# Modulation pieces loaded at once, routing steps put in another order, and the first expert piece drawn ahead, in a two-layer hybrid backbone kernel

## The reference, cut to what matters

```python
for l in range(DEPTH):                                  # DEPTH = 2
    sh1, sc1, g1, sh2, sc2, g2 = split(silu(c) @ w_ada[l] + b_ada[l], 6)
    out = token_mixer(x * (1 + sc1) + sh1)              # w_in, three branches, w_branch, w_o
    x = layer_norm(alpha * x + g1 * out, ln_g[l, 0], ln_b[l, 0])
    ff = hier_moe(x * (1 + sc2) + sh2)
    x = layer_norm(alpha * x + g2 * ff, ln_g[l, 1], ln_b[l, 1])
def hier_moe(h):                                        # 4 groups x 8 experts, d_ff 256
    p_g, g_sel = top_k(softmax(h @ w_coarse), 1)        # one group for a token
    top_v, top_i = top_k(fine logits of that group, 2)  # two experts in it
    hid = silu(h @ w1[e]) * (h @ w3[e])                 # for every expert e
    y = sum over e of (hid * gate[:, e]) @ w2[e]
```

## Time and profile before

| | us |
|---|---|
| median of three timed runs | 1419.67 |
| lowest, highest | 1418.65, 1422.27 |
| profiled execution | 1415.51 |
| its span, first to last instruction | 1412.7 |

### The profile page before, as it was taken

The page is one execution under the profiler, slowest core; times in us unless marked ns, Lnnn a source line. Parts: engine busy times, 40 slices in busy tenths (PEclk is TensorE's granted clock), DMA queues, the critical chain, the costliest instruction groups (busy, mean ns, idle before and its releaser), DMA issues.

```text
span 1412.7 us, 17444 instructions
## 1 busy us (share of the span) xinstructions
PE 1301.1 (92%) x6488; PEld 1028.0 (73%) x6488; DVE 997.4 (71%) x1119; ACT 734.1 (52%) x693; POOL 85.0 (6%) x97
## 2 busy tenths in 40 slices
PE   3699999999879999999969999999987999999994
PEld 0577777887568787888747777788776778788873
DVE  0455556678468888888877466666855888888886
ACT  0424443563246767667653335345424666676772
POOL 4000000000200000000033000000020000000000
PEclk9999998999979999999989999998985999999998
DMA  9767663435749989999956757432434899999991
GB/s 338 267 214 261 243 244 114 127 119 191 293 179 329 340 319 330 332 336 343 350 169 229 282 211 266 149 121 96 138 135 151 276 333 328 337 333 322 341 359 50
DMA packets 96274, 349.53 MB, mean 247 GB/s; under 512 B 8580, under 2 KB 12064, under 8 KB 79792
## 3 DMA queue, kind: packets, MB, share of 16 engines
q1 hardware_dynamic: 87792, 299.32, 59.6%
q0 software_dynamic: 8384, 48.96, 9.9%
HBM read 345.58 MB, written 3.70 MB: 247 GB/s over the span
## 4 chain that ended last, share of the span: by engine, by line
PE 72%; DVE 15%; DMA 5%; ACT 3%; issue 3%; DVEq 2%; ACTq 0%; SPq 0%
PE bank L817 68%; DVE wl L1592 7%; PE bank L820 4%; DMA raw<-in_w_ada 2%; ACT wh L1530 1%; DMA raw<-in_w_in 1%; DVE tmp L1592 1%; DMA adaw<-in_w_ada 1%; DVE merged L1592 1%; ACT wh L1321 1%; DVE hTl L1592 1%; DMA raw<-in_moe_w 1%; DVE hid L2227 0%; DVE x2l L1592 0%; DVE gv L1592 0%
## 5 line engine op out<-in xcount | busy, mean ns | idle before, releaser
L1592 DVE TENSOR_TENSOR wl<-raw,wh 128x2048 fp32r<-128x2048 f32 (+1 forms) x268 | 612.2, 2284 | 163.4 <-ACT wh L1321 104.6
L1530 ACT ACTIVATE wh<-raw 128x2048 fp32r<-128x2048 f32 x192 | 367.3, 1917 | 53.8 <-PE bank L817 43.8
L817 PE MATMUL bank<-wh,xgh 128*128 128x512 f32 x512 | 212.3, 415 | 0.0
L817 PE MATMUL bank<-wh,hTh 128*128 128x512 f32 (+1 forms) x480 | 196.8, 410 | 12.8 <-DVEq L1690 8.3
L817 PE MATMUL bank<-wh,xgl 128*128 128x512 f32 x512 | 204.8, 400 | 0.0
L817 PE MATMUL bank<-wl,xgh 128*128 128x512 f32 x512 | 204.3, 399 | 0.0
L817 PE MATMUL bank<-wl,hTh 128*128 128x512 f32 (+1 forms) x480 | 192.0, 400 | 0.0
L817 PE MATMUL bank<-wh,hTl 128*128 128x512 f32 (+1 forms) x480 | 191.6, 399 | 0.0
L1321 ACT ACTIVATE wh<-raw 128x2048 fp32r<-128x2048 f32 (+1 forms) x76 | 142.2, 1873 | 82.9 <-PE bank L817 68.2
L817 PEld LDWEIGHTS bank<-wh,hTh 128*128 128x128 f32 x480 | 95.8, 200 | 35.7 <-issue 7.1
L817 PEld LDWEIGHTS bank<-wh,xgl 128*128 128x128 f32 x512 | 97.6, 191 | 23.7
(11 more groups left out here) (275 smaller groups left out, 1624.1 us busy)
## 6 DMA issues: line engine op xcount, KB each, us to landing
raw<-in_moe_w SPq DMA_DIRECT2D x256, 512.0 KB, 4.7
raw<-in_moe_w SPq DMA_DIRECT2D x64, 1024.0 KB, 5.3
raw<-in_w_in SPq DMA_DIRECT2D x52, 1024.0 KB, 5.3
adaw<-in_w_ada POOLq DMA_DIRECT2D x32, 1024.0 KB, 6.9
raw<-in_w_ada SPq DMA_DIRECT2D x16, 1024.0 KB, 8.7
raw<-in_w_branch SPq DMA_DIRECT2D x12, 1024.0 KB, 5.3
raw<-in_w_o SPq DMA_DIRECT2D x8, 1024.0 KB, 4.8
lnrow<-in_ln_rows POOLq DMA_DIRECT2D x4, 1024.0 KB, 6.4
```

The costliest lines, as they stand in the source:

```text
L817: return behind(nc.tensor.matmul(*args, **kw))
L1530: tally(A_(wh[c][:, :], raw[:, r, :], ACT.Copy), part_high[c])
L1592: return V.tensor_tensor(o, a, b, op)
```

## The change

Line numbers of the changed kernel are those of its own file.

- **Modulation pieces.** Four of the eight pieces stay in `raw` slots; the other four get buffers of their own. In the opening SP issues them in the first batch, and POOL issues nothing but three small transfers before they have landed. For layer 1, POOL issues its four behind the mixer's last use of those buffers, and `lnrow` waits until they are used.
- **Opening.** In layer 0 x is turned before the last two modulation pieces, and the mod columns are formed before piece 0 is split. q goes stream 0 half 0, stream 0 half 1, stream 1 half 0, stream 1 half 1; in layer 1 stream 1 is turned between the first two. ACT does its second tile of stream 1 before it needs DVE's.
- **Norm.** DVE finishes stream 0's factors before stream 1's product; the low part of layer 1's first tile comes before stream 1's scaling.
- **POOL's apply** goes; DVE does the same operations (`complete`): four in experts 2 to 5 of each layer, and four between the ropes of layer 1.
- **Routing.** The second turn-back stands behind `rank`. The low part of expert piece 0 comes before the logits' copy. The second half of the routing (`finish_routing`) moves behind the flag, into the expert stream, and the fifth gather and the modulation turn behind the first expert's `up`. The four zero matmuls go; the first `scatter` starts the banks.
- **Arms.** On PE, ACT and SP the single-round arm comes first. On DVE the order of the arms stays.

```diff
 def layer_pieces(l):
-    out = ada(0, 0) if l == 0 else []
+    out = ada(0, 0, 0, SLOTS) if l == 0 else []
...
-    out += following[:7] + [("router",)] + following[7:]
+    out += following[:SLOTS] + [("router",)]
...
+            if straight:
+                with eng.If(more < 1):
+                    stream(single, 0, True)
+                with eng.Else():
+                    both()
...
             for i in range(SLOTS):
                 load(0, i)
+            load_first(0)
+            load_first(1)
             sp.dma_start(cst[:, :], A["consts"]).then_inc(once, 16)
...
+            load(0, SLOTS)
+            load_first(2)
+            load_first(3)
...
+            for i in range(DC - SLOTS):
+                pool.wait_ge(first_in[i], 16)
...
-                apply(l, 0)
-                pool.wait_ge(x_full, 4 * l + 2)
+                if l < L - 1:
+                    pool.wait_ge(turned_low, 10 * l + 10)
...
+                    for i in range(DC - SLOTS):
+                        pool.dma_start(late[i][:, :], w[:, SLOTS + i, 0:PIECE]).then_inc(late_in[i], 16)
...
-                turn_x(l, "x1T")
-                for key in "qkv":
+                else:
+                    turn_x(l, "x1T", (0,))
+                for n in range(4):
+                    s, h = n // 2, n % 2
+                    if n == 1 and l:
+                        turn_x(l, "x1T", (1,))
+                    project_half(l, ("q", h), h, ["q0", "q1"], (s,))
+                for key in "kv":
                     simple(l, key)
...
                     for i in range(NE):
                         up(i)
+                        if i == 0:
+                            gather(tally, rnd, 0, PREP - 1)
+                            if rnd == 0 and l < L - 1:
+                                turn_mod(l, 0, "adaT_next")
...
-                    product(1)
                     invert(0)
...
+                    product(1)
                     spread(1)
...
+                def complete(n, s, k):
+                    if s == k == 0:
+                        dve.wait_ge(lnload, (2 * l + 1 - n) * 16)
+                    tt(x[:, s, :], x[:, s, :], lnrow[:, k, :], ALU.add if k else ALU.mult)
+                    return drain()
...
                 rows("x2T", 1)
+                lower(Tally(dve), 0, 0)
...
-                    piece(0)
-                    for j in range(2, PREP):
-                        gathered(0, j)
                     piece(1)
-                    piece(2)
+                    gathered(0, 2)
+                    gathered(0, 3)
+                    if rnd == 0:
+                        finish_routing()
+                        weigh(tally, 0)
+                    gathered(0, 4)
...
+                        if rnd == 0 and 2 <= i < 6:
+                            done = complete(0, i // 2 - 1, i % 2)
```

More of the change, by code:

```diff
@@ L460, in hybrid_backbone @@
         slot_free = [sem(f"slot_free{i}") for i in range(SLOTS)]
+        first = (first0, first1, first2, first3)
+        first_in = [sem(f"first_in{i}") for i in range(DC - SLOTS)]
+        late = (first0, first1, first2, late3)
+        late_in = [sem(f"late_in{i}") for i in range(DC - SLOTS)]
         ada_full = [sem(f"ada_full{i}") for i in range(2)]
@@ L608, in rounds, with both @@
             more = eng.value_load(need[0:1, 0:1], min_val=0, max_val=1)
-            rest, skipped = Tally(eng), Tally(eng)
-            with eng.If(more > 0):
-                stream(rest, 0, False)
-                begin(skipped, 1)
-                stream(skipped, 1, True)
-            for b, n in freed:
-                skipped.amount(free[b], n)
-            with eng.Else():
-                stream(Tally(eng, rest, skipped), 0, True)
+            single, first, second = Tally(eng, counts), Tally(eng), Tally(eng)
+            def both():
+                stream(first, 0, False)
+                begin(second, 1)
+                stream(second, 1, True)
+            if straight:
[4 more added lines that the diff above has]
+            else:
+                with eng.If(more > 0):
+                    both()
+                with eng.Else():
+                    stream(single, 0, True)
+            for s, n, m in counts:
+                m -= sum(k for b, k in freed if free[b] is s)
+                assert (single.of(s), first.of(s), second.of(s)) == (n, n, m)
         @block.sync
@@ L677, in _ @@
                 more = sp.value_load(need[0:1, 0:1], min_val=0, max_val=1)
-                with sp.If(more > 0):
-                    expert_loads(l, 0, SLOTS, len(BODY))
-                    expert_loads(l, 1, 0, len(BODY))
-                    for i in range(SLOTS if l < L - 1 else 0):
-                        load(l + 1, i)
-                with sp.Else():
+                with sp.If(more < 1):
                     expert_loads(l, 0, SLOTS, len(BODY))
@@ L689, in _ @@
                             load(l + 1, i)
+                with sp.Else():
+                    expert_loads(l, 0, SLOTS, len(BODY))
+                    expert_loads(l, 1, 0, len(BODY))
+                    for i in range(SLOTS if l < L - 1 else 0):
+                        load(l + 1, i)
             sp.wait_ge(out_ready, 1)
@@ L705, in _ @@
             pool.dma_start(lncol[:, :, :, :, :], A["ln_rows"].rearrange("l n k (p c) -> p l n k c", c=DC)).then_inc(bada_in, 16)
-            def apply(l, n):
-                to, which = (l, "x2T") if n == 0 else (l + 1, "x1T")
-                pool.wait_ge(lnload, (2 * l + n + 1) * 16)
-                for s in range(2):
-                    bank_full(pool, to, f"{which}{s}1")
-                    pool.tensor_tensor(x[:, s, :], x[:, s, :], lnrow[:, 0, :], ALU.mult)
-                    pool.drain()
-                    pool.tensor_tensor(x[:, s, :], x[:, s, :], lnrow[:, 1, :], ALU.add)
-                    pool.drain().then_inc(x_full, 1)
+            for i in range(DC - SLOTS):
+                pool.wait_ge(first_in[i], 16)
             for n in range(L):
@@ L836, in accumulate @@
                     w, freed = (adaw0, adaw1)[k % 2], ada_free[k % 2]
+                elif at == 0 and c >= SLOTS:
+                    pe.wait_ge(first_in[c - SLOTS], 16)
+                    w, freed = first[c - SLOTS], None
+                elif c >= SLOTS:
+                    pe.wait_ge(late_in[c - SLOTS], 16 * at)
+                    w, freed = late[c - SLOTS], None
                 else:
@@ L1274, in scatter @@
                                     fills(ins, f"moe{s}{n}")
-                    for j in range(PREP):
+                    for j in range(PREP - 1):
                         gather(tally, rnd, 0, j)
@@ L1355, in modulate @@
                     high(0, 1)
+                    rows(1, 1)
+                    act.drain().then_inc(s1_act, 1)
                     if n == 0:
@@ L1358, in modulate @@
                     high(1, 0)
-                    rows(1, 1)
-                    act.drain().then_inc(s1_act, 1)
                     high(1, 1)
@@ L1782, in _ @@
                 if l == 0:
+                    modulation(l, 0, "adaT0")
                     convert_to(0, 0)
[L1784 to L1785 removed]
+                if l == 0:
+                    low(0, 0)
+                else:
+                    convert_to(l, 1)
+                low(0, 1)
                 rows("x1T", 0)
[L1787 removed]
                 low(1, 0)
```

231 lines of the change are left out of this document (135 added, 96 removed).

## The result

The changed kernel takes 1403.76 us (median of four runs, 1400.20 to 1404.46) against 1419.16 of the kernel before (four runs): ratio 0.9895, 95% interval [0.9869, 0.9921], or 14.9 us less by the ratio. Forecast were 12.9 less and 1407. The profiled execution went from 1415.51 to 1404.46, its span from 1412.7 to 1402.7, so the two traces show 10.0 of it.

What follows compares the result with a forecast made beforehand. TensorE was taken as the bound (72% of the chain, busy 92%), so only its gaps give time. Terms -8 - 5 - 5.5 - 3 + 8.6 = -12.9 gave 1402.6 profiled, 1407 us as median; range 1397 to 1417.

Steps and rivals of the forecast that it cites:

- Opening: Kernel start to first projections: modulation columns 12.3 us earlier, new q order costing 4.3; -8 us (bounds -4, -11).
- Walks: Mixer to experts: earlier flags and first expert matmuls; -5 us in layer 0, -5.5 in layer 1 (bounds -1, -8 each).
- Opening of layer 1: Start of layer 1: q starts earlier and GpSimd no longer stretches VectorE's splits; -3 us (bounds 0, -5).
- Expert loop: Experts 2 to 5, both layers: VectorE's added operations, 1.32 us each, are barely hidden; +8.6 us (bounds +3, +10.6).
- Rival 1: Expert loop: the eight operations are hidden, costing +3 us or less; total 1401 us; chance 0.16.
- Rival 4: Experts 2 to 5, both layers: VectorE paces, late splits delay loads; slower, 1425 us; chance 0.08.
- Rest: Removed zero matmuls, memset and semaphores, and the second lnrow load: 0 us.
- Rival 2: Opening: stays bound by transfers at 332 GB/s and gives only 2 us; total 1413 us; chance 0.13.
- Rival 3: Mixer to experts: VectorE ends each walk where it did, terms fall to -1 to -2; 1415 to 1417 us; chance 0.09.

Runs made afterwards that it cites:

- e3: Changed kernel with layer 0's first projection in the old order (half 0 of both streams, then half 1 of both): ratio 0.9873.
- e10: Changed kernel with the old four-slot opening loads and TensorE order, GpSimd still held until the eighth modulation piece landed: ratio 0.9866.
- e5: Changed kernel with the two-round arm first again on TensorE, ScalarE and SyncE: ratio 0.9971.
- e7: Changed kernel with the norm's old order, stream 1's product before stream 0's factors are inverted: ratio 0.9925.
- e2: Changed kernel with GpSimd's scaling of x restored and VectorE's eight replacement operations removed: ratio 0.9866.
- e8: Changed kernel with VectorE's two casts of gathered tokens ahead of piece 1's low part, and its single-round arm first: ratio 0.9940.
- e4: Changed kernel, but GpSimd no longer waits for the first modulation pieces before its small transfers: ratio 0.9978.
- e9: Kernel before the change, with GpSimd held after three small transfers until the eighth modulation piece has landed: ratio 0.9906.
- e6: Changed kernel with the routing's second half and first gate selection ahead of the flag again on VectorE, ScalarE's second exponential too: ratio 0.9976.
- e12: Changed kernel with e10's opening, casts first with VectorE's far arm, and loop operations moved to experts 9, 10, 17 and 18: 1386.88 us, ratio 0.9794.

## Why the prediction was right, and where its steps were not

The time, its sign and the rough size held. That the number is so near is in part luck, twice. By the places of the two traces the walks gave 3.0 more than forecast and the loops cost 3.2 more, which cancel; the opening gave 1.0 less, the opening of layer 1 0.6 more, and the mixers and the tail, put at nothing, took 1.9 and 0.3. That makes 10.0 of the 12.9. And the profiled execution came at 1404.5 for the 1402.6 of the sum; the 4.2 that stood between profile and median before, and that the forecast carried over, was -0.7 this time.

- **Opening, -8 forecast.** The places came as worked out: the last piece 32.2 (32), T 37.7 (37.5), first projection 41.0 (40.6), a pause of 3.57 (about 4). The copy of v gained 7.0. The missing 1 is the size of the last term: the new order of q was put at 4.3 and cost 5.5 (e3), twelve more matmuls and a second slow stretch behind the pause (14 matmuls at 0.44 each, granted clock 0.50). What the term got right by its sum it did not name: the working's 11.2 MB ahead of the last piece leave out GpSimd's 2.7 MB without a word and credit the hold with the step from 33.7 to 32 alone. The runs gave the hold 9.0. The extra buffers and the new order of q, which seemed to carry the gain, cost 2.2 (e10 beside e3) and 5.5 (e3), by TensorE's last matmul of v.
- **Walks, -5 and -5.5.** Measured -6.5 and -7.0. The step that failed is "Near arms can help TensorE and ScalarE by 0 to 4, but VectorE ends last; cost of the edit 0". With the far arms the two walks are 9.7 longer (e5). VectorE does end last, but it waits for ScalarE's conversion of piece 1, that stands behind the gathered tokens, and these behind TensorE's arm. The 4.30 of idle time on TensorE's gather stood in the earlier trace rows; the prediction allowed 0 to 4 for it, set it at nothing, and credited the move of the routing with what needs both edits.
- **Opening of layer 1, -3.** Measured -3.6, or -3.3 by TensorE's last matmul of v. The start of q behind the last `hid` is 3.3 earlier too, as worked out (726.5 for 729.78). The norm's order is 1.4 of it (e7) and GpSimd's operations are 1.0 (e2); the rest, the order of q and of the turn of x, was not run alone.
- **Expert loop, +8.6.** Measured +11.8, of which the operations are 11.2 (e2). From hid to hid 10.74 in expert 3 against the 10.6 forecast, 4.6 over four experts. The term was short because it ended with expert 5: the splits stay late behind it, and another 1.1 is lost by expert 8. Rival 1 (hidden) is refuted. Rival 4's mechanism is partly there: VectorE was the pacer, and the loads did come late behind it (ScalarE waited up to 2.67 for one in layer 0 and up to 2.07 in layer 1), at about 1 a layer and not the 5 that the rival added. How much of that 1.1 is the loads' and how much the splits' own lateness isn't separated.
- **Rest, 0.** The tail moved by 0.3. The ISA-cache rule of the Trainium skill (Advanced Engine Details and Errata, ISA Cache), which I priced at 0.7 on ScalarE at the end of its near arm, cost nothing there: its table load waits 0.29 for nothing visible, and its wait for VectorE stayed at 3.03 (3.27 before). On VectorE, where e8 put it to the test, the same jump cost 4.86 and 3.29. So the two engines don't agree, and that these waits are code being loaded is not shown by any run.
- **Rival 2** (the opening stays bound by transfers, 1413) would have come true without the hold, and more: in e4 the opening gives nothing, and 0.9978 is 1416. **Rival 3** (the loop not brought forward) would have come true by its time with either the arms or the routing left: 0.9971 and 0.9976 are 1415 and 1415.8.
- **Rate.** The queues moved 11.35 MB in the first 32 us, 355 GB/s with the slow start in it, and 406 GB/s between 20 and 34. The 358 GB/s of the Trainium skill (SBUF — State Buffer, in its section on the bandwidth-pool intuition) was no ceiling here.

## What to carry to other kernels

Where a first result waits for a load, look at who else has bytes in the queues, the small transfers of another engine above all, and hold them back before adding buffers: here one wait was worth as much as the whole change. When two waits lie side by side, taking away one of them gains next to nothing, and the gain comes with the second; so price an edit with its neighbour in place and gone. Price a branch at both of its ends, on each engine apart: the near arm was worth 9.7 on the side of TensorE, ScalarE and SyncE, and cost 7.9 on VectorE.

## What the runs showed of the hardware

- A GpSimd operation on 128x1024 holds a VectorE TENSOR_TENSOR whose two inputs both lie in SBUF: 2.10 for 16 elements that take 0.17 otherwise (it ends at 378.87, GpSimd's at 378.85), 3.34 for a split of 2.29. Steps beside it that read a PSUM bank kept their time: in e2 the `x2l<-bank,x2h` at 382.50, beside a GpSimd operation of 382.12 to 384.48, took its usual 0.69.
- Behind a far jump TensorE stood for 3.4 to 4.3 before its first matmul in six cases (both layers of the kernel before, e9 and e5), and in one of them a second time, 4.60 inside a row of 16 matmuls; VectorE for 3.3 to 4.9 (the kernel before, e6, e8, e12).
- GpSimd's 2.7 MB in small transfers took 20% of the queues' time, SP's 11.2 MB took 76%.
- The granted clock of the same mixer code was 0.97 in one trace and 0.93 in another, and the stretch 134.66 and 140.94 us.
- TensorE went at the slow step (0.43 to 0.44) twice in the changed kernel's opening, behind pauses of 4.01 and 3.57. The second slow stretch, 14 matmuls, is one that the kernel before didn't have behind its pause of 1.10.
